# A 31-tap depthwise convolution moved from VectorE and GpSimd to TensorE, in a two-layer decoder step

## The reference, cut to what matters

```python
def conformer_conv(pa, buf, conv_w, conv_b, ln_g, ln_b):
    val, gate = jnp.split(pa, 2, axis=-1)
    a = val * jax.nn.sigmoid(gate)
    xpad = jnp.concatenate([buf.astype(a.dtype), a], axis=1)
    y = causal_depthwise(xpad, conv_w) + conv_b.astype(a.dtype)
    y = jax.nn.silu(layer_norm(y, ln_g, ln_b))
    return y, xpad[:, -(CONV_A_W - 1):]
```

## Time and profile before

| what | value |
|---|---|
| runs | 1164.25, 1164.42, 1167.72 us, median 1164.42 |
| profiled execution, its own time | 1169.0 us |
| its span, first to last instruction | 1167.2 us |
| mean granted PE clock | 0.969 |
| PE busy | 1113.7 us, 95% |
| DVE busy | 744.7 us, 64% |
| ACT busy | 563.7 us, 48% |
| POOL busy | 358.3 us, 31% |
| the mixer's input projection, layer 0 | from about 215 us to 349 us of the span |

### The profile page before, as it was taken

The page is one execution under the profiler, slowest core; times in us unless marked ns, Lnnn a source line. Parts: engine busy times, 40 slices in busy tenths (PEclk is TensorE's granted clock), DMA queues, the critical chain, the costliest instruction groups (busy, mean ns, idle before and its releaser), DMA issues.

```text
span 1167.2 us, 26164 instructions
## 1 busy us (share of the span) xinstructions
PE 1113.7 (95%) x9072; PEld 1075.8 (92%) x9072; DVE 744.7 (64%) x982; ACT 563.7 (48%) x900; POOL 358.3 (31%) x449
## 2 busy tenths in 40 slices
PE   6999999888999999999989999998999999999996
PEld 6999999788899899999889999997888989999995
DVE  5666643889865766654566665349877566666446
ACT  5544444652256654454454445446412566444444
POOL 3222211337823332221122222114574242222112
PEclk9999999998899999999999999999978899999998
DMA  7654467242325365444435545654323255554552
GB/s 259 214 183 180 168 198 238 97 156 91 109 91 182 124 201 183 179 168 181 160 129 182 183 181 176 214 189 145 110 82 110 82 166 181 181 180 175 185 182 74
DMA packets 64746, 188.72 MB, mean 162 GB/s; under 512 B 9594, under 2 KB 20866, under 8 KB 64514
## 3 DMA queue, kind: packets, MB, share of 16 engines
q1 hardware_dynamic: 64642, 187.38, 46.8%
HBM read 183.97 MB, written 3.38 MB: 161 GB/s over the span
## 4 chain that ended last, share of the span: by engine, by line
PE 84%; DVE 7%; issue 6%; ACT 2%; DMA 1%; DVEq 0%; SPq 0%; POOL 0%; ACTq 0%; POOLq 0%
PE ub L289 17%; PE ub L290 16%; PE ub L291 16%; PE quad L289 8%; PE quad L290 8%; PE quad L291 7%; PE mb L595 2%; DVE resid L948 2%; DVE z_t L945 2%; PE mb L628 1%; PE ub L309 1%; PE ub L311 1%; PE ub L310 1%; DVE w_lo L276 1%; DVE proj L1187 1%
## 5 line engine op out<-in xcount | busy, mean ns | idle before, releaser
L276 DVE TENSOR_TENSOR w_lo<-raw,w_hi 128x1024 fp32r<-128x1024 f32 x339 | 449.1, 1329 | 373.0 <-ACT w_hi L270 372.2
L270 ACT ACTIVATE w_hi<-raw 128x1024 fp32r<-128x1024 f32 x339 | 346.4, 1028 | 300.8 <-PE ub L291 211.5
L289 PE MATMUL ub<-hg_hi,w_hi 128*128 128x264 f32 x960 | 283.8, 296 | 1.7 <-DVE proj L1187 1.6
L290 PE MATMUL ub<-hg_lo,w_hi 128*128 128x264 f32 x960 | 278.7, 290 | 0.0
L291 PE MATMUL ub<-hg_hi,w_lo 128*128 128x264 f32 x960 | 278.0, 290 | 0.0
L289 PE MATMUL ub<-act_hi,w_hi 128*128 128x264 f32 x704 | 200.5, 285 | 0.0
L289 PE MATMUL quad<-hg_hi,w_hi 128*128 128x264 f32 x688 | 197.0, 286 | 3.2 <-DVE w_lo L276 3.2
L291 PE MATMUL ub<-act_hi,w_lo 128*128 128x264 f32 x704 | 199.6, 284 | 0.0
L290 PE MATMUL ub<-act_lo,w_hi 128*128 128x264 f32 x704 | 199.1, 283 | 0.0
L290 PE MATMUL quad<-hg_lo,w_hi 128*128 128x264 f32 x688 | 195.6, 284 | 0.0
L291 PE MATMUL quad<-hg_hi,w_lo 128*128 128x264 f32 x688 | 195.3, 284 | 0.0
(11 more groups left out here) (253 smaller groups left out, 1481.9 us busy)
## 6 DMA issues: line engine op xcount, KB each, us to landing
raw<-in_w_gu SPq DMA_DIRECT2D x179, 512.0 KB, 3.4
raw<-in_w_dn SPq DMA_DIRECT2D x64, 512.0 KB, 3.7
raw<-in_w_in SPq DMA_DIRECT2D x44, 512.0 KB, 3.3
raw<-in_w_dn SPq DMA_DIRECT2D x32, 384.0 KB, 3.3
raw<-in_w_out SPq DMA_DIRECT2D x16, 512.0 KB, 3.3
pages<-in_cache_k SPq DMA_DIRECT2D x32, 128.0 KB, 2.2
pages<-in_cache_v SPq DMA_DIRECT2D x32, 128.0 KB, 2.8
con<-in_con SPq DMA_DIRECT2D x1, 1444.0 KB
```

The lines of the kernel that those rows point to most:

```text
L270: eng.activation(w_hi[:, slot, 0:w], raw[:, slot, 0:w], ACT.Copy).then_inc(*sig("hi_ready", reps))
L276: eng.tensor_tensor(w_lo[:, slot, 0:w], raw[:, slot, 0:w], w_hi[:, slot, 0:w].bitcast(F32), ALU.subtract)\
L289: eng.matmul(out, a_hi, x_hi[:, k0 + k, :], start=(first and k == 0), stop=False)
L290: eng.matmul(out, a_hi, x_lo[:, k0 + k, :], start=False, stop=False)
```

## The change

The 31 taps become matrix products. A stationary block of 128 x 32 holds, for 32 channels and four neighbouring taps, a diagonal of tap weights for each tap (`cw`; POOL builds all 64 blocks per layer in one instruction, by multiplying a 32 x 32 identity with a small table `acm`). The moving operand `xs` holds the same 32 channels four times on the partitions, shifted by 0, 1, 2 and 3 tokens. Sixteen transfers from `a_pad` make it, 8 in SP's step 11 and 8 in step 12, each 32 partitions x 572 values. Eight such products of 256 columns accumulate the 32 taps (one is zero), for 4 groups of 32 channels and 2 tiles: 64 matmuls per layer, placed after the first `decode_scores` of unit 14. ACT adds the bias and takes the result out. The sigmoids go from step 10 to step 8, and for that gate B's columns are projected before the values of A. Mean and variance go from after units 21 and 23 to after units 16 and 18.

```diff
-ALR, FG, BQ, BK, AV, AG, BG, BV, DQ, DKK, DVV, CB, CC, CX = 0, 1, 2, 3, 4, 6, 8, 10, 12, 14, 16, 18, 19, 20
+ALR, FG, BQ, BK, AG, BG, AV, BV, DQ, DKK, DVV, CB, CC, CX = 0, 1, 2, 3, 4, 6, 8, 10, 12, 14, 16, 18, 19, 20
...
-A_DVE = 20
+SHIFTS, STEPS = 4, 8
+XW = TP + SHIFTS * STEPS
+XS = 2 * XW - SHIFTS
...
+        cw = proj[:, DVV:24, :].rearrange("p a b -> p (a b)")[:, 0:64 * 32].rearrange("p (c j q m) -> p c j q m", c=2, j=STEPS, q=4)
+        xs = sb("xs", [P, 4, XS])
...
+                if 11 <= n < 13:
+                    if n == 11:
+                        sp.wait_ge(*at(l, "a_in", 1))
+                    for s in (2 * (n - 11), 2 * (n - 11) + 1):
+                        for q in range(4):
+                            sp.dma_start(xs[32 * s:32 * s + 32, q, :], a_flat[32 * q:32 * q + 32, s:s + XS]).then_inc(*sig("xs_in", n=16))
...
+            def conv_taps(l):
+
+                after(l, xs_in=16 * 4 * SHIFTS, a_cw=1, b_vt=1)
+                for c in range(2):
+                    for j in range(STEPS):
+                        for q in range(4):
+                            t = c * XW + SHIFTS * j
+                            mm = pe.matmul(mb[2][32 * q:32 * q + 32, c * TP:(c + 1) * TP], cw[:, c, j, q, :], xs[:, q, t:t + TP],
+                                           start=j == 0, stop=j == STEPS - 1)
+                mm.then_inc(*sig("a_conv"))
...
                 if n == 14:
                     gla_updates(l)
                     decode_scores(l, 0)
+                if n == 14:
+                    conv_taps(l)
                 if n == 15:
                     decode_scores(l, 1)
                 if n == 16:
+                    conv_sum(l)
                     gla_outputs(l)
...
                 if n == 18:
+                    conv_var(l)
                     fox_scores(l, 0)
...
                     decode_outputs(l, (0, 1, 2, 3))
-                    conv_sum(l)
...
-                    conv_var(l)
...
-                if n == 10:
+                if n == 8:
 
                     act.preload_act_table(ACT.Sigmoid)
-                    after(l, proj=10)
+                    after(l, proj=8)
...
+                if n == 15:
+
+                    after(l, a_conv=1)
+                    for c in range(2):
+                        act.activation(ymix[:, YA + c, 0:TP], mb[2][:, c * TP:(c + 1) * TP], ACT.Identity,
+                                       bias=par[:, PAR["acb"] + c:PAR["acb"] + c + 1]).then_inc(*sig("a_all"))
...
-                if n in TAPS:
-                    conv_taps(l, *TAPS[n])
...
+                    pool.tensor_tensor(cw[:, :, :, :, :].rearrange("p c j q m -> p (c j q) m"),
+                                       const("eye", 32).unsqueeze(1).to_broadcast([P, 64, 32]),
+                                       par[:, PAR["acm"]:PAR["acm"] + 64].unsqueeze(2).to_broadcast([P, 64, 32]), ALU.mult).then_inc(*sig("a_cw"))
...
-                    after(l, a_sg=1, past=PAST)
-                    pool.tensor_tensor(a_pad[:, :, TAPS_A - 1:], proj[:, AV:AV + 2, 0:TP], proj[:, AG:AG + 2, 0:TP], ALU.mult).then_inc(*sig("a_in"))
+                    after(l, a_sg=1, past=PAST, proj=10)
+                    pool.tensor_tensor(a_pad[:, :, TAPS_A - 1:TAPS_A - 1 + TP], proj[:, AV:AV + 2, 0:TP], proj[:, AG:AG + 2, 0:TP], ALU.mult).then_inc(*sig("a_in"))
...
-                if n in (13, 15, 17):
```

## The result

| | before | after |
|---|---|---|
| median of the runs | 1164.4 us | 1198.7 us |
| lowest and highest | 1164.25 and 1167.72 (4 runs) | 1197.19 and 1201.17 (4 runs) |
| profiled execution, its own time | 1169.0 us | 1198.6 us |
| its span | 1167.2 us | 1196.8 us |
| mean granted PE clock | 0.969 | 0.961 |

The changed kernel is slower: ratio 1.027, interval 1.024 to 1.031. Of all 53 executions of the kernel before, here and beside the experiments, one took 1982 us at a granted clock of 0.83 and is left out of every ratio. The forecast was 1187 in a range of 1170 to 1205. The sign and the range hold, and the size is short: 22.6 us forecast, 34.3 between the medians, 29.6 between the two profiled executions.

A forecast was written before the change was run, and what follows sets the result against it. PE, busy 95% of the span, was taken as the bound. Per layer 8.0 + 4.4 + 1.0 - 0.9 - 1.2 = 11.3 us, 22.6 for two, took the 1164.4 us median to 1187, range 1170 to 1205.

The forecast's parts named there:

- Part 1: After the first `decode_scores`: 64 matmuls added to PE, overlapping at 90% of four, +8.0 us per layer.
- Part 2: Mixer's start: POOL building `cw` stops DVE, +4.4 us per layer, plus 1.0 for PE's clock in unit 4.
- The lower bound of 2.2: Mixer's start: least cost in us per layer of POOL's building, if DVE and POOL share.
- Part 3: Units 12 to 14: transfers delay the loads of units 15 and 16, removed taps free waits; net -0.9 us per layer.
- The loads arrive in time: Rival, loads of units 15 and 16: no delay, -5.6 us per layer instead of -0.9, time 1178 us; 15%.
- Part 4: From unit 15 on: half clock passes to the convolution, sum unchanged; `conv_sum` behind unit 16 gains, -1.2 us per layer.
- that of the quarters: Rival, the 64 products: no four-way overlap; pairs cost 16.1 us (1203), one by one 28.9 (1229); 12%.
- the hidden building: Rival, mixer's start: only POOL's building of `cw` is hidden, 5.4 us per layer go, time 1176 us; 6%.
- The one on the faster side: Rival, units 14 to 16: clock holds, loads in time, building behind other work; -2.4 us per layer, 1160 us; 7%.

The follow-up runs named there:

- both shifts: Changed kernel with its transfers moved to SP's steps 13 and 14 and POOL building `cw` at the layer's start in its own buffer: 1172.1 us, ratio 1.005.

## Why the prediction came out as it did

Per layer the forecast was 11.3 us, and the two layers gave 16.2 and 14.2. By its own steps:

**Part 1, the products: mechanism right, price too high.** Forecast 8.0, with 7.2 as the least; 64 products cost 6.9 us at full clock. Two things were off. The 0.452 for a full product is a mean that contains the last instruction's own time of each run; within a run it is 0.432. And the quarters overlap four times, not 90% of it: 0.432 against 0.108. From the products' start to the second call it is 12.32 us against 4.47 before, with unit 15 in both, which is 7.9 more and looks like the forecast. That is luck: of the 1.0 beyond the price 0.6 is clock (0.81 granted over the 12.32 us, 0.62 over the 4.47).

The Trainium skill, "TensorE: Matmul & The Clock Gate", section "Measured speedup vs the span model", has 79% of perfect overlap for three tiles. For four tiles in turn the trace shows more: 0.432 against 0.108 is all of it. The 9.1 us that the prediction worked out from that page were 2.2 too many.

**Part 2, the blocks: right mechanism, a little large.** Forecast 4.4 + 1.0; the instruction took 3.65 us, and its early building gave back 4.2 per layer net (5.3 with the wait at layer 1's start added back, 3.2 and 3.9 by stretch A of the profiles). I reckon with 4.2. PE's wait behind it was 1.9 us, and unit 4 ran at 0.50 from 229.4 to 232.8, as forecast.

The Trainium skill, "SBUF — State Buffer", section "Who interferes with whom", says that such a vector instruction and a GpSimd one exclude each other for the whole instruction. The two rests that end 1.08 us after POOL, behind instructions of 3.65 and 2.93 us, agree, and so does the clearing that took 2.93 us and not 1.95. The lower bound of 2.2 is excluded.

**Part 3, the transfers: chain right, size wrong.** The chain was right link by link (load 15 late, ACT waits, DVE's rest stands before the mask, PE waits behind unit 12, none before `decode_scores`). Three links were too short. The first transfer went out at 258.84, not 255.8; PE itself was 2.3 us later by then (unit 12 ended at 266.97 against 264.67), so 0.7 of it is new. The 8 issues, forecast at 0.62 us each, took 6.4 us up to the load behind them, not 5.0. "3.3 us from issue to landing" was 4.4 up to ACT. Not all of that is the transfers' doing: in this execution the loads of the feed-forwards, far from any transfer, also took a median of 4.0 us to land and not 3.4. PE waited 6.5 us, not 3.1. Stretch A is 5.9 us longer on average; less 4.2 for part 2 that leaves +1.7 per layer where the forecast was -0.9, so 2.6 were missed. The gain that it ate was well judged: -5.6 forecast, -6.3 measured with both shifts. "The loads arrive in time" was the wrong rival by this. The experiment that makes it true gave 1180.4, and the rival said 1178, but that is luck: the rival starts from 1187 and gains 4.7 per layer, the experiment from 1198.7 and gains 9.2.

**Part 4, the clock: the step that failed most.** "The first 3 us at half clock pass from the one to the other, and the sum stays", and -1.2 for `conv_sum`. `conv_sum` did fall from 2.11 to 1.05 us. But over stretch B the clock cost 12.1 and 13.1 us against 8.1 and 12.1, 2.5 per layer more, where the forecast gave a gain of 1.2. The work there was 6.8 more per layer, where the forecast had 8.0. The clock's part does not come from the products alone: with both shifts the same 64 products stand there, and the clock costs 7.7 and 12.0. There the sum does stay, and only the gain of 1.2 is missing. What brings the 2.5 in the changed kernel is open. The delays of parts 2 and 3 ahead of the stretch may do it, but with the transfers alone moved it is still 12.1 and 12.0, and there is one profile of each kernel.

The four add up: 11.3 - 1.2 (products) - 1.2 (blocks) + 2.6 (transfers) + 3.7 (clock) = 15.2, the mean of the two layers. Over both layers that is 30.4 us, and 0.8 came back elsewhere, which gives the 29.6 between the profiles. So the forecast of 22.6 is as near as it is because two terms were too large and two too small.

The rest up to 34.3 lies in the choice of the starting point. The profile of before was 4.6 us above the median, and I subtracted that. The profile of after was at its median. The kernel before has no fixed time to this precision: its later medians were 1166.1, 1167.7, 1166.2 and 1165.8 us, with single runs from 1157.5 to 1171.7. What varies is the clock. Over those 48 executions the span goes from 1155.7 to 1169.9 us, while span times granted clock stays between 1128 and 1134: the shortest had 0.977, the longest 0.966. The profile shows the same inside one execution, since stretch B of before has the same work in both layers (81.9 and 81.1) and loses 8.1 us to the clock in one and 12.1 in the other. All four executions of after lost 42 to 47 us to the clock in this way, those of before 26 to 40, so the changed kernel's larger loss over the whole execution is no accident of one profile.

Of the rivals, that of the quarters falls by the 0.108, and the hidden building by DVE's 4.35. The one on the faster side fails at its last condition. With both shifts, the loads come in time and the building is out of the way, and the kernel is still 4.4 us above before. That holds although stretch A gained 6.3 per layer. PE has 6.8 us more to do per layer, and no clock came back for it. Against the kernel with moved taps, both shifts are 18 us slower: by the profiles some 13 us of work in the two stretches B, 2 us of waiting at layer 1's start, and most of the rest clock.

## What to carry to other kernels

Where one engine is busy for 95% of the time, over 100 us of work taken from the others is worth only the waits that it stood in (here 6.3 us per layer), and moving that work two steps later may give all of it for two edited lines. Before adding DMA issues to the queue that feeds the bound engine, add up wait, issues and landing against the lead of the next load: the same 16 transfers cost 9 us less per layer two steps later. And split a stretch into length times granted clock and the rest before explaining it, because work is the same from layer to layer and the clock is not.

## What the runs showed of the hardware

- Four 32-column quarters of the array take float32 products in turn at 0.108 us for 256 columns. One quarter alone takes 0.432, and so does a product of all 128 columns. The narrow product alone saves nothing, and four side by side cost no more than one.
- SP issued 8 transfers of 32 partitions x 572 values in 6.23 us, and the next 8 in 4.94, so the pace isn't constant: 0.78 and 0.62 us each. A 512 KB load behind the first eight needed 4.4 us to reach ACT, the one behind the second eight 3.8, where 3.3 is the median to landing before. How much of that the transfers ahead of them did, no run tells: the median landing of the feed-forwards' loads was 3.4 us in one execution (before) and 3.6 to 4.0 in all others.
- POOL built 2048 values with both operands broadcast in 3.65 us: 1.78 ns a value, less than the 2.15 of the 512-value instruction of the earlier trace rows.
- DVE's rest and POOL's instructions hold each other up: a rest of 1.20 us lasted 4.35 beside the building, and the clearing of 1.95 us lasted 2.93 with a rest in its midst.
- With taps moved, the 16 products of 2 columns of a call took 4.37 and 3.71 us. Both calls in a row took 10.61, at a mean granted clock of 0.66, and the kernel's time was the same.
